# Feed-forwards and conv mixer of a two-layer decoder step as one level of Strassen block products

## The chip, the cores and the metric

One core of a Trainium2 chip runs the whole step in one launch. The metric is the device time of one execution in microseconds. Each time is the median of the runs shown with it; the profile is of one further execution.

## What is computed

Two groups of tokens (1024 prompt tokens; 8 sequences of 4 sample tokens) go through two layers with shared weights. What matters here is the part behind attention:

```python
def conv_mixer(h, prefix, w_in, conv_k, w_out):
    bg, cg, hv = jnp.split(h @ w_in, 3, axis=-1)
    u = cg * hv
    up = jnp.concatenate([prefix.astype(u.dtype), u], axis=1)
    y = sum(conv_k[j] * up[:, j:j + T] for j in range(CONV_WIDTH))
    return (bg * y) @ w_out, up[:, up.shape[1] - (CONV_WIDTH - 1):]

def swiglu(h, w_gu, w_down):
    g, u = jnp.split(h @ w_gu, 2, axis=-1)
    return (jax.nn.silu(g) * u) @ w_down
...
        hp = rms_norm(yp, norm2_g[i]) * (1.0 + sc2p) + sh2p
        yp = yp + g2p * swiglu(hp, ffn_w_gu[i], ffn_w_down[i])
```

Layer 0 is attention and a feed-forward, layer 1 the conv mixer and a feed-forward, then a last RMSNorm. D_MODEL is 1024, D_FF 2816, all in float32. The samples have the same formulas with their own conditioning.

## The kernel before

Model features lie on the 128 partitions (KT = 8 tiles), the 1056 tokens (T) along the free axis, in three chunks (NCH) of 352 (CH). float32 products are made of three fp32r products: weight and token are each split into a high part (an ACT copy to fp32r) and a low part (GpSimd: raw minus high), and `product` (L363 to L370, matmuls on L368) issues high x high, high x low and low x high for each k-tile into one PSUM bank.

The weights stream through a ring of four 128x1024 slots: SP loads `wraw` (`load_w`, L335; in the feed-forward loop L2280), ACT makes `uhi` (`split_hi`, L353), GpSimd makes `ulo` (`split_lo`, L360). Down weights have slots of their own (`draw`, `dhi`, `dlo`; L551, L556, L561).

Every engine runs its own program in the order in which it is written; semaphores tie them. Stages: projection, attention, `pe_out` (L2123: output projection, 24 items, item 16 on are the last), then `pe_ffn` (L2307) for ffn0, `pe_conv` (L2528), `pe_ffn` for ffn1, `pe_end` (L2719). A feed-forward has 11 iterations, each of two tiles of 128 hidden features: six units of a gate and an up product of 24 matmuls (`pe_ffn_unit`), then 24 down products of 6 matmuls (`pe_down`). ACT takes the gate from PSUM through SiLU (L2341), VectorE multiplies by up (L2452), ACT and GpSimd split the result (L2343, L2396), and VectorE adds the down product times the gate vector into the residual `y` in SBUF (`dve_down`, L582 to L591). The conv mixer has four such iterations of three products a tile (`pe_conv_unit`), with the three taps on VectorE (L2653, L2655).

The norm before a stage is made chunk by chunk under the products around it: squares on ACT (L395, L2157), sums over features by float32 matmuls with a matrix of ones (L407), mean (L471), root (L475) and reciprocal (L479), scale (L498), affine and high part on ACT (L522, L525), low part on GpSimd (L534, samples L539). At the end, nine token tiles are turned by matmuls (L2714), scaled from PSUM by VectorE (L2729) and ACT (L2736), and stored.

Of the kernel before, what the change touches and what calls it, by code (L numbers as in the profile page):

```python
# [14 lines left out]
P = 128  # L22
# [40 lines left out]
UP0 = {}  # L63
_at = 0
for _name, _n in (("proj", N_PROJ), ("out", N_OUT), ("ffn0", N_FFN), ("conv", N_CONV), ("ffn1", N_FFN)):
    UP0[_name] = _at
    _at += _n
MM0 = {"proj": 0, "out": 54, "ffn0": 54 + 3 * KT, "conv": 54 + 3 * KT + 6 * FT, "ffn1": 54 + 12 * KT + 6 * FT}
IT0 = {"ffn0": 0, "conv": 3 * FT, "ffn1": 3 * KT + 3 * FT}
# [82 lines left out]
CK0 = {"ffn0": 0, "conv": FT // 2, "ffn1": KT // 2 + FT // 2}  # L152


def program(nc, x_prompt, x_sample, c_prompt, c_sample, cache_k, cache_v, cache_kidx, state_conv, page_table,
# [6 lines left out]
    q_scr = nc.dram_tensor("q_scratch", [P, KT, T], F32, kind="Internal").ap()  # L162

    with ExitStack() as ctx:
# [6 lines left out]
        def layout(*specs):  # L171

            with ExitStack() as inner:
                return [inner.enter_context(nc.sbuf_tensor(n, s, d)) for n, s, d in specs]


        ident = sb("ident", [P, P])
        rotm = sb("rotm", [P, P])
# [2727 lines left out]
```

## Time and profile before

| | |
|---|---|
| median of 3 runs | 2795.92 us (2793.12 to 2799.52) |
| span of the profiled execution | 2797.2 us |
| from the first ffn0 product to the end | about 821 us to 2797 us of that span |
| busy share PE, PEld, VectorE, ACT, GpSimd | 97%, 89%, 42%, 30%, 33% |
| DMA, mean over the span | 69 GB/s |

PE is TensorE's matmuls, PEld its weight loads, DVE VectorE, POOL GpSimd, SPq the queue from which SyncE issues transfers. A group's "busy" counts each instruction from its start to its modelled end, so overlapping matmuls count twice; intervals between starts are the pace. "Idle before" is the time in which the engine had nothing to do before such an instruction, with what released it.

### The profile page before, as it was taken

The numbers are of one execution on the slowest core, as the hardware profiler recorded it, in microseconds if no ns is written. First come the engines' busy times: TensorE is split into PE (matmuls) and PEld (weight loads), VectorE is DVE, ScalarE is ACT, GpSimd is POOL, SyncE is SP. The second block draws the span as 40 slices with busy tenths as digits, with TensorE's granted clock in tenths as the row PEclk, the third lists the DMA queues.
The fourth block names the chain that finished last, engine by engine and source line by source line (L and its number), as shares of the span: only waits on it lengthen the run. The fifth ranks groups of instructions, "written<-read, shape, count | busy, mean of one in ns | idle before, by whom it ended". The sixth has DMA issues, their size and how long they took to land.

```text
span 2797.2 us, 46769 instructions
## 1 busy us (share of the span) xinstructions
PE 2711.9 (97%) x17946; PEld 2482.8 (89%) x17946; DVE 1173.9 (42%) x2915; ACT 850.2 (30%) x1622; POOL 919.6 (33%) x714
## 2 busy tenths in 40 slices
PE   6989999999999999999999999999999999999999
PEld 4848865767789999999999899999899999999999
DVE  5488988663263222222222443333622222222233
ACT  4156656772162111111111521111611111111113
POOL 3414643351054222222222533223532222222221
PEclk8999999999999999999999999999999999999999
DMA  8305567004321111111111012102111111111101
GB/s 305 84 24 164 172 235 224 2 1 134 99 76 46 46 45 45 45 45 45 45 45 45 16 45 61 46 16 61 46 46 45 45 45 45 45 45 45 45 15 64
DMA packets 206062, 192.23 MB, mean 69 GB/s; under 512 B 32480, under 2 KB 183880, under 8 KB 205418
## 3 DMA queue, kind: packets, MB, share of 16 engines
q1 hardware_dynamic: 205930, 190.42, 22.5%
q8 instruction: 88, 1.44, 0.2%
q14 instruction: 44, 0.36, 0.0%
HBM read 175.43 MB, written 14.96 MB: 68 GB/s over the span
## 4 chain that ended last, share of the span: by engine, by line
PE 88%; DVE 5%; ACT 2%; DMA 2%; issue 1%; POOL 1%; SPq 1%; DVEq 0%; ACTq 0%
PE PS L368 74%; PE PS L1880 3%; PE PS L1909 2%; PE PS L1891 2%; DVE s_all L1577 1%; DVE na L498 1%; PE PS L888 1%; DMA adaw<-in_ada_w_dram 1%; PE PS L407 1%; PE PS L901 1%; PE PS L2714 1%; ACT na L522 1%; PE PS L1896 1%; PE PS L1922 1%; POOL hlo L534 0%
## 5 line engine op out<-in xcount | busy, mean ns | idle before, releaser
L368 PE MATMUL PS<-hhi,uhi 128*128 128x352 f32 (+1 forms) x3240 | 1062.4, 328 | 19.2 <-DVE hlo L1306 7.3
L368 PE MATMUL PS<-hhi,ulo 128*128 128x352 f32 (+1 forms) x3240 | 1044.9, 323 | 0.0
L368 PE MATMUL PS<-hlo,uhi 128*128 128x352 f32 (+1 forms) x3240 | 1043.9, 322 | 0.0
L368 PEld LDWEIGHTS PS<-hhi,uhi 128*128 128x128 f32 (+1 forms) x3240 | 610.2, 188 | 39.3 <-issue 25.8
L368 PEld LDWEIGHTS PS<-hlo,uhi 128*128 128x128 f32 (+1 forms) x3240 | 612.0, 189 | 3.5 <-issue 0.2
L368 PEld LDWEIGHTS PS<-hhi,ulo 128*128 128x128 f32 (+1 forms) x3240 | 610.5, 188 | 0.8
L2396 POOL TENSOR_TENSOR alo<-af,ahi 128x352 fp32r<-128x352 f32 x132 | 126.0, 954 | 1023.1 <-ACT ahi L2343 1023.1
L2452 DVE TENSOR_TENSOR af<-sg,PS 128x352 f32<-128x352 f32 x132 | 68.8, 521 | 878.0 <-PE PS L368 872.6
L368 PE MATMUL PS<-ahi,dhi 128*128 128x352 f32 x1248 | 417.8, 335 | 4.7 <-DVE y L591 3.8
L368 PE MATMUL PS<-ahi,dlo 128*128 128x352 f32 x1248 | 402.6, 323 | 0.0
L368 PE MATMUL PS<-alo,dhi 128*128 128x352 f32 x1248 | 401.5, 322 | 0.0
L360 POOL TENSOR_TENSOR ulo<-wraw,uhi 128x1024 fp32r<-128x1024 f32 x124 | 294.8, 2397 | 65.4 <-ACT uhi L353 65.3
L582 DVE SCALAR_TENSOR_TENSOR y<-PS,mod,y 128x352 f32<-128x352 f32 x416 | 242.7, 584 | 157.2 <-PE PS L368 157.2
L2341 ACT ACTIVATE sg<-PS 128x352 f32<-128x352 f32 x132 | 61.3, 465 | 680.4 <-PE PS L368 680.4
L368 PEld LDWEIGHTS PS<-ahi,dhi 128*128 128x128 f32 x1248 | 233.8, 187 | 34.0 <-DVE y L591 26.8
L368 PEld LDWEIGHTS PS<-alo,dhi 128*128 128x128 f32 x1248 | 235.1, 188 | 2.2
L368 PEld LDWEIGHTS PS<-ahi,dlo 128*128 128x128 f32 x1248 | 234.4, 188 | 0.0
L2343 ACT ACTIVATE ahi<-af 128x352 fp32r<-128x352 f32 x132 | 65.8, 498 | 506.4 <-DVE af L2452 506.4
L585 DVE SCALAR_TENSOR_TENSOR y<-PS,mod,y 128x320 f32<-128x320 f32 x208 | 114.2, 549 | 48.6 <-PE PS L368 40.6
L353 ACT ACTIVATE uhi<-wraw 128x1024 fp32r<-128x1024 f32 x124 | 124.1, 1045 | 4.7 <-issue 4.7
L561 POOL TENSOR_TENSOR dlo<-draw,dhi 128x1024 fp32r<-128x1024 f32 x52 | 123.9, 2406 | 0.3 <-ACT dhi L556 0.2
L534 POOL TENSOR_TENSOR hlo<-na,hhi 128x352 fp32r<-128x352 f32 (+1 forms) x72 | 71.7, 996 | 119.6 <-ACT hhi L525 119.1
(303 smaller groups left out, 2817.0 us busy)
## 6 DMA issues: line engine op xcount, KB each, us to landing
wraw<-in_ffn_w_gu_dram SPq DMA_DIRECT2D x88, 512.0 KB, 7.4
wraw<-in_ada_w_dram SPq DMA_DIRECT2D x80, 512.0 KB, 4.5
draw<-in_ffn_w_down_dram SPq DMA_DIRECT2D x44, 512.0 KB, 4.3
wraw<-in_conv_w_in_dram SPq DMA_DIRECT2D x24, 512.0 KB, 7.1
adaw<-in_ada_w_dram SPq DMA_DIRECT2D x16, 512.0 KB, 14.4
wraw<-in_attn_w_out_dram SPq DMA_DIRECT2D x48, 128.0 KB, 3.1
y_scratch<-y SPq DMA_DIRECT2D x1, 4224.0 KB, 12.7
xst<-in_x_prompt_dram SPq DMA_DIRECT2D x4, 1024.0 KB, 8.5
```

Of the source, the lines that this page charges most:

```text
L353: act.activation(uhi[:, u % WR, :, 0:cols], wraw[:, slot, :, 0:cols], ACT.Copy).then_inc(up_hi, 1)
L360: pool.tensor_tensor(ulo[:, u % WR, :, 0:cols], wraw[:, slot, :, 0:cols], uhi[:, u % WR, :, 0:cols].bitcast(F32), ALU.subtract).then_inc(u ...
L368: last = pe.matmul(out, w(kt), x(kt), start=(n == 0), stop=(n == 3 * count - 1))
L534: pool.tensor_tensor(hlo[:, ft, cols_of(n)], nbufs(q)[1][:, k % 2, 0:width(n)], hhi[:, ft, cols_of(n)].bitcast(F32), ALU.subtract).then_in ...
L561: pool.tensor_tensor(dlo[:, b, :], draw[:, b, :], dhi[:, b, :].bitcast(F32), ALU.subtract)\
L582: dve.scalar_tensor_tensor(out=y[:, m, chunk(n)], in0=b[:, 0:CH], scalar=gate(m)[:, 0:1], in1=y[:, m, chunk(n)], op0=ALU.mult, op1=ALU.add ...
L585: dve.scalar_tensor_tensor(out=y[:, m, 2 * CH:SEQ], in0=b[:, 0:PC], scalar=gate(m)[:, 0:1], in1=y[:, m, 2 * CH:SEQ], op0=ALU.mult, op1=ALU ...
L1880: last = pe.matmul(wide(2 * g)[:, c], q_of(i, t)[64 * g:64 * g + 64], kT[64 * g:64 * g + 64, t // 4, c], start=True, stop=True)
L2341: act.activation(sg[:, p, :], bank[2 * p][:, 0:CH], ACT.Silu).then_inc(silu_rdy, 1)
L2343: act.activation(ahi[:, jj, chunk(n)], af[:, p, :], ACT.Copy).then_inc(act_hi, 1)
L2396: pool.tensor_tensor(alo[:, jj, chunk(n)], af[:, k % 2, :], ahi[:, jj, chunk(n)].bitcast(F32), ALU.subtract)\
L2452: dve.tensor_tensor(af[:, p, :], sg[:, p, :], bank[2 * p + 1][:, 0:CH], ALU.mult).then_inc(act_f, 1)
```

## The change

The three stages behind the output projection ("phases" ffn0, conv, ffn1) are rewritten for all engines. The constants now cut tokens into two groups of 528 (GS), each in two halves of 264 (H), and weights into two by two blocks. A two by two block product is made of seven products (the Winograd form), accumulated in PSUM in the order ORD with takes between: in all, an item has seven positions.

- A *U item* (up side) makes a pair of 128-feature tiles of gate or up (conv: c, h, b) for both halves of both token groups; PE runs 4 k-blocks x 3 matmuls x groups per position, 264 columns each. In the first and the last pair of a phase it is one item for each token group.
- Weight blocks of position 2 to 5 are sums made by VectorE (`dve_sums`); each position's 128x512 block is split by ACT (`act_split`) and GpSimd (`pool_split`) into one of four ring slots, four positions ahead. `lo_engine` gives all low parts to GpSimd but the first four of conv and ffn1.
- Results are taken by ACT (copies) and VectorE (adds, products) into rows of `y`, which is spilled to DRAM meanwhile (`sp_spill`) and reloaded (`sp_back`).
- The product of gate and up is cut into seven token pieces (`act_piece`, `pool_piece`, `dve_token_sums`), stored to DRAM through two stage buffers (`sp_piece`) and reloaded as tokens of the down side (`sp_tokens`).
- A *D item* (down side) makes half of the output features for four hidden tiles; feed-forwards have five chunks of two items, conv one. The hidden tiles left over are plain products (items P and Z, `pe_plain`, twelve matmuls each). At ffn's end that is one pair.
- The tokens of the next phase are built from the residual, 7 combinations by 4 k-blocks with high and low parts: group 0 during and behind Z (`act_z`, `dve_z`, `pool_z`), group 1 during the first pair's group 0 items (`act_build`, `dve_build`, `pool_build`). For ffn0, group 0's stand in `dve_out_proj`, `act_out_proj` and `pool_out`. The sums of squares move from PE to GpSimd (`pool_add`) with one small float32 product for each group (`pe_sum`).
- The tail's nine tiles are made in Z and behind it.

The diff, cut to its core:

```diff
-UP0 = {}
-_at = 0
...
+H = T // 4
+GS = 2 * H
+LAST = SEQ - GS
+ORD = (1, 2, 6, 5, 7, 3, 4)
+T_AT = {4: 0, 5: 1, 6: 2, 7: 3, 1: 4, 2: 5, 3: 6}
...
+PHASES = ("ffn0", "conv", "ffn1")
+KINDS = {"ffn0": "gu", "conv": "chb", "ffn1": "gu"}
+N_PAIRS = {"ffn0": FT // 2, "conv": KT // 2, "ffn1": FT // 2}
+N_CHUNKS = {"ffn0": 5, "conv": 1, "ffn1": 5}
...
+def lo_engine(p):
+
+    it, pos = ITEMS[PREP[p][0]], PREP[p][1]
+    if it.stage != "U":
+        return "pool"
+    first = IN_PHASE[it.phase][0].prep
+    if p < first + 4:
+        return "dve" if it.phase else "pool"
+    return "pool"
...
+                _who = ("act", "dve", "act", "act", "dve", "dve", "act" if _it.kind in "gc" else "dve")[_u]
...
+        def pe_u_item(pe, it):
+            fresh = it.at == 0 and it.kind == FIRST_KIND[it.phase]
+            for pos, i in enumerate(ORD):
+                r, w = it.res + pos, slot_of(it.prep + pos)
+                pe_split_ready(pe, it.prep + pos)
+                pe_bank_free(pe, r)
+                for s in it.groups:
+                    out, x = PS[:, 2 * SET[r] + s, 0:H], th[s][:, :, T_AT[i]]
+                    for k in range(4):
+                        if fresh:
+                            pe_tokens_ready(pe, it.phase, s, k, i)
+                        hi, lo = w[:, RH, P * k:P * k + P], w[:, RL, P * k:P * k + P]
+                        pe.matmul(out, hi, x[:, TH, k, :], start=(k == 0 and i in (1, 2, 5)), stop=False, skip_group_check=True)
+                        pe.matmul(out, hi, x[:, TL, k, :], start=False, stop=False, skip_group_check=True)
+                        last = pe.matmul(out, lo, x[:, TH, k, :], start=False, stop=(k == 3), skip_group_check=True)
+                last.then_inc(r_mm, 1)
...
+        def act_piece(act, n, k):
...
+            act.wait_ge(rd_d, PAIR_END[ph, j, 1 if s is None else s])
+            after(act, t_st[tp % 2], 16 * (tp // 2))
+            out = stages[tp % 2][:, TH, :]
...
+        def act_u_item(act, it):
+            for pos in range(7):
+                act_piece(act, it.n, pos)
+                act_take(act, it, pos)
+                act_silu(act, it, pos)
+                act_split(act, PREP_AT[it.n, pos])
+                if it.at == 0 and it.groups == (0,):
+                    act_build(act, it.phase, pos + (7 if it.kind in "uh" else 0))
...
+        def pool_split(pool, p):
+            if lo_engine(p) != "pool":
+                return
+            pool.wait_ge(w_hi, p + 1)
+            w = slot_of(p)
+            pool.tensor_tensor(w[:, RL, :], split_source(p), w[:, RH, :].bitcast(F32), ALU.subtract).then_inc(w_lop, 1)
...
+        def pool_build(pool, f, step):
+
+            if f == 0 and step == 0:
+                pool_add(pool, 0, 1, 7)
+            if step in (2, 4, 6, 8):
+                pool_low(pool, f, 1, step // 2 - 1, 1)
+            if step in (3, 5, 7, 9):
+                pool_lows(pool, f, 1, step // 2 - 1, (5, 6, 7, 4))
+
+        def pool_u_item(pool, it):
+            for pos in range(7):
+                pool_piece(pool, it.n, pos)
+                pool_split(pool, PREP_AT[it.n, pos])
+                if it.at == 0 and it.groups == (0,):
+                    pool_build(pool, it.phase, pos + (7 if it.kind in "uh" else 0))
...
+        def dve_t123(dve, f, s, k):
...
+            dve.tensor_tensor(t1, a[:, H:GS], a[:, 0:H], ALU.subtract).then_inc(n_t, 1)
+            dve.wait_ge(n_t, c + 1)
+            dve.tensor_tensor(t2, b[:, H:GS], t1, ALU.subtract).then_inc(n_t, 1)
+            dve.tensor_tensor(a[:, H:GS], b[:, H:GS], a[:, H:GS], ALU.subtract).then_inc(n_t, 1)
...
+        def dve_u_item(dve, it, late):
+
+            for pos in range(7):
+                p = PREP_AT[it.n, pos]
+                dve_split(dve, late)
+                dve_token_sums(dve, it.n, pos)
+                if it.kind == "b" and pos in (0, 2):
+                    dve_taps(dve, it, pos // 2)
+                dve_take(dve, it, pos)
+                dve_sums(dve, p + 1)
+                if it.at == 0 and it.groups == (0,):
+                    dve_build(dve, it.phase, pos + (7 if it.kind in "uh" else 0))
+                late = p
+            return late
...
             act_att(act)
             act_out_proj(act)
-            act_ffn(act, "ffn0", 1, 2, N_FFN + 4)
-            act_conv(act)
-            act_ffn(act, "ffn1", 3, 4, N_FFN)
+            for f in range(3):
+                act_phase(act, f)
             act_end(act)
```

## Rows read from the trace of the kernel before

**Rows 1.** The page's first part: busy time, share and instructions of each engine.

```profile
PE 2711.9 (97%) x17946; PEld 2482.8 (89%) x17946; DVE 1173.9 (42%) x2915; ACT 850.2 (30%) x1622; POOL 919.6 (33%) x714
```

**Rows 2.** The page's fourth part: the chain that ended last, by line.

```profile
PE PS L368 74%; PE PS L1880 3%; PE PS L1909 2%; PE PS L1891 2%; DVE s_all L1577 1%; DVE na L498 1%; PE PS L888 1%; DMA adaw<-in_ada_w_dram 1%; PE PS L407 1%; PE PS L901 1%; PE PS L2714 1%; ACT na L522 1%; PE PS L1896 1%; PE PS L1922 1%; POOL hlo L534 0%
```

**Rows 3.** Windows: stretch; its length, then busy us (instructions); clock, DMA share, GB/s.

```profile
821.00:1590.00 769.00, 766.84 (x4732) 753.01 (x4731) 226.27 (x512) 160.79 (x261) 249.73 (x161) 1.00 0.15 43
1590.00:1640.00 50.00, 45.62 (x262) 42.10 (x261) 31.79 (x61) 27.85 (x52) 22.83 (x21) 1.00 0.23 64
...
2755.00:2797.00 42.00, 36.32 (x287) 35.59 (x285) 19.01 (x47) 15.24 (x27) 6.78 (x8) 1.00 0.29 106
```

**Rows 4.** Timeline of PE (start, us, instruction): first and last of 26 matmuls.

```profile
1107.10 0.32 PE L368 MATMUL PS<-hlo,uhi 128*128 128x352 f32 x1
...
1111.07 0.32 PE L368 MATMUL PS<-hhi,ulo 128*128 128x352 f32 x1
```

**Rows 5.** Timeline of PE: first and last of 22 matmuls of 256 columns.

```profile
213.50 0.28 PE L368 MATMUL PS<-ulo,hhi 128*128 128x256 f32 x1
...
216.01 0.28 PE L368 MATMUL PS<-ulo,hhi 128*128 128x256 f32 x1
```

**Rows 6.** Timeline of ACT: SiLU takes, first and sixth of an iteration, first of the next.

```profile
1107.69 0.47 ACT L2341 ACTIVATE sg<-PS 128x352 f32<-128x352 f32 x1 [24.68 <-PE PS L368]
...
1145.76 0.47 ACT L2341 ACTIVATE sg<-PS 128x352 f32<-128x352 f32 x1 [2.50 <-PE PS L368]
1177.44 0.47 ACT L2341 ACTIVATE sg<-PS 128x352 f32<-128x352 f32 x1 [24.76 <-PE PS L368]
```

**Rows 7.** Timeline of PE in the out stage: sums between items 16, 17 and 18.

```profile
785.42 1.34 PE L407 MATMUL PS<-nsq,ones 128*128 128x352 f32 x4
790.42 1.34 PE L407 MATMUL PS<-nsq,ones 128*128 128x352 f32 x4
```

**Rows 8.** Groups of POOL by form: count, busy us, mean ns, idle before.

```profile
L360 POOL TENSOR_TENSOR ulo<-wraw,uhi 128x1024 fp32r<-128x1024 f32 x124 | 294.8, 2397 | 65.4 <-ACT uhi L353 65.3
L2396 POOL TENSOR_TENSOR alo<-af,ahi 128x352 fp32r<-128x352 f32 x132 | 126.0, 954 | 1023.1 <-ACT ahi L2343 1023.1
```

**Rows 9.** Groups of ACT by form.

```profile
L353 ACT ACTIVATE uhi<-wraw 128x1024 fp32r<-128x1024 f32 x124 | 124.1, 1045 | 4.7 <-issue 4.7
L2343 ACT ACTIVATE ahi<-af 128x352 fp32r<-128x352 f32 x132 | 65.8, 498 | 506.4 <-DVE af L2452 506.4
```

**Rows 10.** Groups of DVE by form.

```profile
L582 DVE SCALAR_TENSOR_TENSOR y<-PS,mod,y 128x352 f32<-128x352 f32 x416 | 242.7, 584 | 157.2 <-PE PS L368 157.2
L479 DVE RECIPROCAL rstd<-rstd 128x352 f32<-128x352 f32 x9 | 21.2, 2351 | 5.6 <-ACT rstd L475 5.6
```

**Rows 11.** Timelines of DVE (first row) and of POOL (the others) in the out stage.

```profile
793.15 2.69 DVE L498 TENSOR_TENSOR na<-y,rstd 128x352 f32<-128x352 f32 x1 [0.96 <-POOL hlo L534]
...
792.09 0.95 POOL L534 TENSOR_TENSOR hlo<-na,hhi 128x352 fp32r<-128x352 f32 x1 [0.53 <-ACT hhi L525]
793.05 2.41 POOL L360 TENSOR_TENSOR ulo<-wraw,uhi 128x1024 fp32r<-128x1024 f32 x1
795.40 1.22 POOL L534 TENSOR_TENSOR hlo<-na,hhi 128x352 fp32r<-128x352 f32 x1
```

**Rows 12.** Single lines L498 and L2452: duration min/median/max ns, first and last start.

```profile
L498 DVE TENSOR_TENSOR na<-y,rstd x72: 477/522/2685, 783.8 to 2020.5; 128x352 f32<-128x352 f32 x48, 128x320 f32<-128x320 f32 x24
...
L2452 DVE TENSOR_TENSOR af<-sg,PS x132: 520/522/523, 832.4 to 2752.6; 128x352 f32<-128x352 f32 x132
```

**Rows 13.** The chain that ended last, in order of time: start, us, what.

```profile
2782.18 10.84 PE PS L2714 x96
```

**Rows 14.** Windows, columns as in rows 3: a stretch after thin PE work.

```profile
388.00:400.00 12.00, 9.49 (x57) 4.25 (x57) 5.89 (x30) 4.53 (x21) 3.37 (x9) 0.51 0.97 357
```

**Rows 15.** DMA issues: count, KB each, median us to landing.

```profile
y_scratch<-y SPq DMA_DIRECT2D x1, 4224.0 KB, 12.7
...
q_scratch<-qst_ SPq DMA_DIRECT2D x21, 176.0 KB, 2.4
```

More of the change, by code:

```diff
@@ L62 @@
     _at += _n
-UP0 = {}
-_at = 0
[L65 to L69, printed above, removed]
+UP0 = {"proj": 0, "out": N_PROJ, "ffn0": N_PROJ + N_OUT}
+MM0 = {"proj": 0, "out": 54, "ffn0": 54 + 3 * KT}
 TOK = (0, P, CH - P)
@@ new lines, with outline @@
+Item = namedtuple("Item", "n phase stage kind at e groups prep ring res")
+PHASES = ("ffn0", "conv", "ffn1")
+KINDS = {"ffn0": "gu", "conv": "chb", "ffn1": "gu"}
+N_PAIRS = {"ffn0": FT // 2, "conv": KT // 2, "ffn1": FT // 2}
+N_CHUNKS = {"ffn0": 5, "conv": 1, "ffn1": 5}
+BOTH = (0, 1)
+def outline(name):
+    kinds, pairs = KINDS[name], N_PAIRS[name]
+    for j in range(pairs):
+        if j == 0 and name == "conv":
+            yield from (("U", k, j, 0, (s,)) for s in BOTH for k in "ch")
+            yield "U", "b", j, 0, BOTH
+        elif j in (0, pairs - 1):
+            yield from (("U", k, j, 0, (s,)) for s in BOTH for k in kinds)
+        else:
+            yield from (("U", k, j, 0, BOTH) for k in kinds)
+    for c in range(N_CHUNKS[name]):
+        yield from (("D", "", c, e, BOTH) for e in range(2))
+    if name == "conv":
+        yield "P", "", 2, 0, BOTH
+    yield "Z", "", pairs - 1, 0, BOTH
@@ new lines @@
+DVE_LO = list(itertools.accumulate(lo_engine(p) == "dve" for p in range(len(PREP))))
+SUM0 = {}
+for _it in ITEMS:
+    if _it.stage in "UD":
+        SUM0[_it.n] = 4 * len(SUM0)
+RAW_COUNT, _c = [], [0, 0]
+for _it in ITEMS:
+    _c[_it.n % 2] += 64 if _it.stage == "D" else 32
+    RAW_COUNT.append(_c[_it.n % 2])
+TAP_END, _c = {}, 0
+for _it in ITEMS:
+    if _it.stage == "U" and _it.kind == "b":
+        for _b in range(2):
+            _c += 3 + (1 if 0 in _it.groups else 0) + (2 if 1 in _it.groups else 0)
+            TAP_END[_it.n, _b] = _c
@@ new lines, with stage_done, v_row, t_op @@
+N_PIECES = _tp
+def stage_done(tp):
+    return [16 * ((tp + 1 - k) // 2) for k in range(2)]
+def v_row(f, pair):
+    return 6 if f == 1 or pair % 2 == 0 else 2
+def t_op(f, j):
+    done = [(g, k) for g in range(3) for k in range(2 * N_CHUNKS[PHASES[g]])]
+    return 4 * done.index((f, j))
+SQ0 = [0, 8, 16, 24, 33, 41, 50, 58]
+FIRST_KIND = {0: "g", 1: "c", 2: "g"}
+def lop(g, k, i):
+    at = (1, 5, 6, 7, 4).index(i)
+    if g == 0:
+        return 4 * k + at + 1 if i != 4 else 16 + k + 1
+    return 20 * g + 5 * k + at + 1
```

1885 lines of the change are left out of this document (1129 added, 756 removed).

## The prediction, made before the change was run

> **What bounds the kernel now.** I read the page's busy shares first: PE is busy 97% of the span, no other engine over 42% [rows 1]. The chain that ended last lies for 74% on the one line that issues every split product, L368 [rows 2]. By stretches, the first feed-forward keeps PE busy 766.8 of 769 us, the seam to the conv mixer 45.6 of 50, the tail 36.3 of 42 [rows 3]. So from 821 us to the end the kernel is matmul issue, and two prices matter: what a product costs PE, and what the other engines need once PE is quicker.
>
> PE's pace: 25 intervals of 352-column matmuls took 3.97 us, 158.8 ns each [rows 4]; 21 of 256 columns took 2.51 us, 119.5 ns [rows 5]. The difference, 39.3 ns for 96 columns, is one column per 0.41 ns; some 13 ns a matmul are fixed. 264 columns then cost 122.9 ns. In an iteration, five 48-matmul units take 38.07 us, the whole 432 take 69.75 [rows 6]; the 144 down matmuls between (69.75 - 38.07 - 7.63 = 24.05) cost 167 ns each, 50 ns extra per group of six.
>
> **The PE term.** Before: 2 x 11 x 69.75 = 1534.5 us for the feed-forwards, and 1728 x 0.159 + 576 x 0.167 = 371 for conv: 1906. After: a product position is 4 k-blocks x 3 matmuls x 2 token groups of 264 columns, 24 matmuls, 2.94 us; seven positions replace eight block products. Feed-forward: 22 item-equivalents x 168 = 3696, D 10 x 168 = 1680, the plain last pair 192: 5568 x 0.1226 = 683, and 140 x 0.05 for D's groups: 690. Conv: 2016 + 336 + 384 = 2736: 338. Together 1718, a gain of 188 us. The seventh of the work saved becomes a tenth of the time, since the fixed 13 ns are now paid 13872 times, not 11808.
>
> The Trainium skill (TensorE: Matmul & The Clock Gate, Back-to-back issue gap) gives columns / 2.4 + 2.5 ns as the isolated gap, 112.5 ns here, by which the PE term would be 144 us lower; it warns that this leaves out weight loads. For 352 columns it gives 149.2 where the row has 158.8, so the rows decide.
>
> **Who takes what else.** In the out stage (L2123) the 20 sums on PE between products go, 1.34 us for four [rows 7]; items 16 to 23 ran every 5.0 us there and need 3.82. I put item 16 at 778.5 and the stage's end at 810 (before: 821.4).
>
> Prices at the new sizes: GpSimd subtract or add, 2.15 ns an element between 352 and 1024: 0.76 us for 264 elements, 1.29 for 512, 1.33 for 528 [rows 8]. ACT copies 0.63 for 512, by the same slope method [rows 9]. VectorE from PSUM 0.78 for 528, reciprocal 1.78 for 264 [rows 10].
>
> The price I think decides: VectorE and GpSimd exclude each other where VectorE reads two SBUF operands. L498, 0.52 us at the median [rows 12], began at 793.15 and took 2.69, while a GpSimd subtract ran from 793.05 to 795.46; then the next GpSimd subtract took 1.22 instead of 0.95 [rows 11]. VectorE needed 0.38 us alone for 352 elements: 0.57 for 528, 0.55 for 512, 0.29 for 264. With one operand in PSUM it never waited: L2452 has 520/522/523 ns [rows 12]. So I add both engines' SBUF work as one queue, "the pair".
>
> The Trainium skill (SBUF — State Buffer, Who interferes with whom) also lets tensor_scalar and copies hold the pair; that would add only conv's first taps, some 8 us of pair time in an item with slack, and no time to the sum.
>
> **Middle pairs.** Per gate/up pair (PE 41.2 us): GpSimd 14 low parts 18.1 and 7 token pieces 9.3; VectorE 8 weight sums 4.4, 4 token sums 2.3, 3 products 1.7. Pair: 35.8, so PE still sets the pace. In the gate half it is 22.8 against 20.6. Following its start from the end of the last up position: five VectorE ops stand ahead of the take of position 1 (two weight sums, three token sums). Each finds GpSimd in a split (1.29) or a piece (1.33): weight sum done 2.55, token sum 4.5, weight sum 6.35, token sums 8.3 and 10.2 (three GpSimd ops between), take 10.9. PE wants that bank for position 3 at 8.8. I take 2 us a pair, 20 pairs: +40. From both sides: 0 (VectorE gets in first) and 3.5 (stores, below).
>
> **First pair of each phase.** Its items run one token group at a time, so weight splits are doubled, and the second group's tokens are built beside the first's products. Up to the second group's first product, GpSimd has 11 splits 14.2 and 20 low tokens 15.2, VectorE 15.5 on the pair (8 scalings 4.6, 12 sums 3.5, four high-low steps 3.4, weight sums and samples 4): 45 us where PE needs 20.6. After it, 14 splits and sums take 24 against 20.6: 3.5.
>
> **Seams.** In Z, VectorE's two reciprocals hold the last banks: 2.6. The next tokens need 20 low parts 15.2, two adds 2.7 and VectorE 10.9 = 28.8 of the pair after Z ends; with the chain scale, affine, high, low at its ends, 31.7 until splits go on. With 6 for dependencies: 2.6 + 31.7 + 45 + 6 + 3.5 - 20.6 = 68 a seam, twice: +136. Bounds: 50 if half of VectorE's work slips in while GpSimd waits for ACT, 85 if each k-block waits for its own chain.
>
> Out to feed-forward: from item 16 on, the pair has GpSimd 39.3 (add 1.3, four out splits 9.6, six adds 8, 20 low tokens 15.2, four splits 5.2) and VectorE 13.2: 52.5, then 46.2 as above. 778.5 + 98.7 + 5 + 3.5 - 20.6 = 865, 55 past the out stage's end. Bounds 40 to 70.
>
> **Last pair of each phase.** Four single-group items, PE 41.2; the pair has 22.8 (seven pieces of the pair before) + 12.1 + 13.9 + 12.1 = 60.9; the ring of four slots absorbs some: +17, conv the same with six items: +51 (36 to 60).
>
> **Tail.** Nine output tiles at 10.84 / 6 = 1.8 us [rows 13] and the last sums: 25 (22 to 30). **Clock.** After thin PE work TensorE's granted clock was 0.51 over 12 us, its lower level of 1.2 GHz [rows 14]; PE idles here at three starts: +8 (0 to 20).
>
> **New waits, and what is queued behind them.** PE waits per position for the low part of its ring slot (w_lop) and for its bank's last taker; all later products stand behind. VectorE waits before a take for ACT's copy of the partner (rd_a); weight sums for later slots stand behind. ACT waits before a token piece for the stage's store; its take, SiLU and split stand behind, and GpSimd's low part behind the split. SP waits for t_lo before a store; weight loads stand behind, needed an item later.
>
> **Edits costed at nothing.** ACT's splits, takes and pieces, 19 of 41.2 us a pair, behind PE; without that cover they would add their excess over 2.94 a position. SP's weight, token and spill transfers, one to four transfers ahead. y's reload, under the last group's items and D. VectorE keeps the first four low parts of phases two and three, inside Z.
>
> **Sum.** 810 + 1718 + 55 + 136 + 51 + 40 + 25 + 8 = 2843 us against this execution's span of 2797.2; the runs' median is 2795.9, so I forecast 2842.
>
> **Rivals.** (1) *The pair does not bind* (other side). If VectorE's short operations fall into GpSimd's waits for ACT, starts and seams are limited by GpSimd alone: the out start 30, seams 40 each, ends 25, middle 0, clock 5: 810 + 1718 + 30 + 80 + 25 + 25 + 5 = 2693; halfway 2768. It decides for faster once these extras come to under 262 us, against my 315. For it: all row averages have GpSimd at 33% [rows 1] with waits rare. Against: with both queued the rows show strict alternation [rows 11]. 0.23. (2) *The store round trip binds the middle.* A token piece's stage buffer returns only after its low part and a 528 KB store. Rows: 176 KB lands in 2.4 us, 4224 KB in 12.7 [rows 15], so 3.4 alone; two weight loads go out beside it. At 6 us the ACT take of position 6 comes 3.5 us late: 20 x 3.5 - 40 = +30 over my sum, and with slower seams +70: 2872 to 2913. For: ACT stands in order behind that wait, takes and splits queued after it. 0.17. (3) *It doesn't do what it says.* Before, all low parts are already on GpSimd, so "instead of VectorE" has no counterpart in this trace; what it adds to the pair is the 0.7 us a block by which GpSimd is slower, about 6 us per first pair, already in the sum. As a case without Strassen's effect I give it 0.02: 2797.
>
> **Chances and range.** Forecast 2843 (its own spread 2785 to 2875) 0.50, of which 0.02 lies on the faster side; rival 1 0.23; rival 2 0.17; within 0.2% 0.05, rival 3 in it; 0.05 slower than rival 2. A measurement of this kernel can tell some 0.2% from no change. Faster 0.25, same 0.05, slower 0.70. Range 2755 to 2935, which cuts the lower half of rival 1.
>
> **What would show it.** PE: L368's groups become 128x264 with starts 123 ns apart; about 2000 more matmuls. Gaps after each Z of 20 to 30 us on PE, released by GpSimd low tokens; in the first items GpSimd near 65% and VectorE ops of 1 to 1.9 us where 0.4 is their own. In a middle gate item one gap of 2 us before position 3, released by VectorE. If the gaps end on a DMA store, rival 2; if VectorE keeps its short durations, rival 1. I am wrong as a whole if PE's pace at 264 columns isn't 123 ns, or if a build takes 30 us, not 45.

## The result, and the profile after

The changed kernel takes 2810.6 us (median; 2803.6 to 2812.0) against 2797.5 us for the kernel before on the same chip, a ratio of 1.0047 (95% interval 1.0035 to 1.0059): slower, as forecast, but by 13 us and not by 45. Below, ratios are always to the kernel before, and 0.01 of ratio is 28 us. The profiled execution's span is 2810.2 us.

The page of the changed kernel: busy times, chain that ended last, then two groups of its fifth part and its two DMA rows of the token store.

```profile
PE 2539.0 (90%) x19876; PEld 2329.1 (83%) x19876; DVE 1862.9 (66%) x3186; ACT 1188.7 (42%) x2295; POOL 1682.9 (60%) x1278
...
PE 60%; DVE 12%; POOL 11%; DMA 6%; issue 5%; ACT 3%; SPq 1%; ACTq 0%; DVEq 0%; POOLq 0%
...
L2468 PE MATMUL PS<-th,ring 128*128 128x264 f32 x3136 | 923.6, 295 | 147.1 <-DVE y L2934 62.9
...
L2763 POOL TENSOR_TENSOR ring<-wraw,ring 128x512 fp32r<-128x512 f32 x364 | 536.5, 1477 | 261.5 <-ACT ring L2571 261.4
...
t_scratch<-stage SPq DMA_DIRECT2D x154, 528.0 KB, 3.1
th<-t_scratch SPq DMA_DIRECT2D x77, 1056.0 KB, 8.4
```

Where PE was busy 97% [rows 1], it is now busy 90%: its busy time fell by 173 us, and its idle time rose from 85 to 271 us. VectorE rose from 42% to 66% and GpSimd from 33% to 60%; the latter's 512-column pass takes 1.48 us on average, where the prediction priced it at 1.29 alone. The chain, which lay for 74% on one product line [rows 2], is now split among PE, VectorE and GpSimd.

Windows of the changed kernel, columns as in [rows 3]. In order: start of the first feed-forward, its middle pairs, its last pair, its down-projections, first pair of the second feed-forward with the seam ahead of it.

```profile
804.00:900.00 96.00, 57.67 (x342) 53.80 (x340) 75.24 (x100) 46.20 (x96) 76.31 (x65) 0.75 0.23 68
900.00:1279.40 379.40, 371.57 (x3025) 369.09 (x3026) 211.86 (x199) 162.67 (x280) 287.42 (x190) 1.00 0.44 141
1279.40:1343.00 63.60, 46.79 (x338) 45.05 (x337) 36.58 (x40) 28.18 (x57) 53.07 (x37) 0.90 0.82 298
1343.00:1550.50 207.50, 207.47 (x1681) 207.50 (x1682) 146.80 (x260) 46.37 (x75) 106.41 (x75) 0.99 0.60 218
...
2011.50:2107.50 96.00, 56.42 (x342) 52.55 (x340) 84.21 (x109) 54.58 (x115) 80.08 (x69) 0.79 0.22 66
```

From these I take an "excess": the time of a stretch less its matmuls at 0.1226 us each. 336 products are 41.2 us, so the start has 54.8 us of excess, the last pair 22.4, the middle 8.6 (3024 products, 370.8). The down-projections have none beyond 1.5 us. Over the up-projections of all three phases (item by item, from PE's timeline) the excess is 126 us in first pairs, 70 in last pairs, 26 in middle pairs. Before, the first feed-forward had 2 us of idle PE in 769 [rows 3].

PE's waits from 740 us on (total us, times, longest) say for whom.

```profile
PE PS L2468 <- DVE y L2934: 62.9, 50, 4.3
PE PS L2468 <- ACT y L2617: 37.9, 28, 4.7
PE PS L2536 <- issue: 28.6, 2, 14.3
PE PS L2468 <- issue: 24.4, 12, 7.4
PE PS L2468 <- POOL ring L2763: 12.4, 10, 4.6
PE PS L2490 <- DVE y L2934: 10.2, 3, 4.6
```

The first two are takes of finished products out of PSUM: in the up-projections PE waits mostly for a bank, not for weights (L2763 is only 12.4). L2536 is the norm's sum between two phases. The last row is the first down-product of each phase, and there the named take is only the last link. In the first feed-forward it stands in VectorE's program behind two weight sums, and these, like ScalarE's and GpSimd's splits of the same weights, waited for a transfer. Rows of ScalarE, VectorE and PE:

```profile
1340.02 1.15 ACT L2571 ACTIVATE ring<-wraw 128x512 fp32r<-128x512 f32 x2 [5.52 <-DMA wraw<-in_ffn_w_down_dram]
1340.03 0.69 DVE L2872 TENSOR_TENSOR sums<-wraw 128x512 f32<-128x512 f32 x1 [3.56 <-DMA wraw<-in_ffn_w_down_dram]
1342.47 0.41 DVE L2934 TENSOR_TENSOR y<-y,PS 128x264 f32<-128x264 f32 x1
1343.03 0.56 PE L2490 MATMUL PS<-th,ring 128*128 128x264 f32 x1 [4.59 <-DVE y L2934]
```

The DMA share is 0.82 over this last pair, where the middle pairs have 0.44. In the second feed-forward the same gap is 4.38 us. These 9 us are counted in the last pairs' 70.

The excess also holds the price of a lower clock. A window of the changed kernel from the end of a 4.30 us gap in the last pair (its row is in experiment 5), columns as above:

```profile
1288.24:1293.50 5.26, 5.26 (x24) 5.26 (x25) 1.22 (x1) 2.39 (x5) 5.26 (x5) 0.52 0.53 200
```

Here 24 matmuls took 219 ns each and not 122, at a granted clock of 0.52, the lower level of 1.2 GHz. In PE's timeline 132 intervals of the last pairs are of this kind (195 to 250 ns, no gap), 12.5 us together above 122.6 ns each; 276 are in first pairs (26.5 us) and 54 in middle pairs (4.3 us).

The pace itself: first and last row of 41 consecutive matmuls in PE's timeline.

```profile
1199.82 0.28 PE L2469 MATMUL PS<-th,ring 128*128 128x264 f32 x1
...
1204.70 0.28 PE L2470 MATMUL PS<-th,ring 128*128 128x264 f32 x1
```

4.88 us for 40 intervals: 122.0 ns for 264 columns, where [rows 4] and [rows 5] had given 122.9. The Trainium skill (TensorE: Matmul & The Clock Gate, Back-to-back issue gap) would have 112.5 by its formula for the isolated gap; the trace doesn't agree with it here.

### The profile page after: what moved, and what is told of

It is laid out like the page before. It is cut to its first block, busy times and chain, and to the rows that moved or that the text cites. A ratio compares the mean times of both kernels' runs of the same rounds, so it can differ in the third digit from the quotient of the medians.

```text
span 2810.2 us, 51944 instructions
## 1 busy us (share of the span) xinstructions
PE 2539.0 (90%) x19876; PEld 2329.1 (83%) x19876; DVE 1862.9 (66%) x3186; ACT 1188.7 (42%) x2295; POOL 1682.9 (60%) x1278
## 4 chain that ended last, share of the span: by engine, by line
PE 60%; DVE 12%; POOL 11%; DMA 6%; issue 5%; ACT 3%; SPq 1%; ACTq 0%; DVEq 0%; POOLq 0%
PE PS L572 9%; PE PS L2468 7%; PE PS L2470 7%; PE PS L2469 7%; PE PS L2490 5%; PE PS L2492 5%; PE PS L2493 5%; POOL ring L2763 5%; POOL stage L2776 4%; DMA t_scratch<-stage 3%; PE PS L1818 2%; PE PS L1847 2%; PE PS L1829 2%; POOL th L2791 2%; DVE s_all L1515 1%
## 5 line engine op out<-in xcount | busy, mean ns | idle before, releaser
L2468 PE MATMUL PS<-th,ring 128*128 128x264 f32 x3136 | 923.6, 295 | 147.1 <-DVE y L2934 62.9
L2470 PE MATMUL PS<-th,ring 128*128 128x264 f32 x3136 | 910.6, 290 | 0.0
L2469 PE MATMUL PS<-th,ring 128*128 128x264 f32 x3136 | 910.5, 290 | 0.0
L2468 PEld LDWEIGHTS PS<-th,ring 128*128 128x128 f32 x3136 | 610.3, 195 | 169.2 <-issue 134.9
L2763 POOL TENSOR_TENSOR ring<-wraw,ring 128x512 fp32r<-128x512 f32 x364 | 536.5, 1477 | 261.5 <-ACT ring L2571 261.4
L2469 PEld LDWEIGHTS PS<-th,ring 128*128 128x128 f32 x3136 | 611.3, 195 | 0.3
L2470 PEld LDWEIGHTS PS<-th,ring 128*128 128x128 f32 x3136 | 610.7, 195 | 0.0
L2763 POOL TENSOR_TENSOR ring<-sums,ring 128x512 fp32r<-128x512 f32 x269 | 408.9, 1524 | 197.5 <-ACT ring L2571 197.4
L2934 DVE TENSOR_TENSOR y<-y,PS 128x528 f32<-128x528 f32 (+1 forms) x207 | 122.9, 594 | 412.0 <-PE PS L2470 402.1
L2490 PE MATMUL PS<-th,ring 128*128 128x264 f32 x1232 | 353.4, 287 | 10.2 <-DVE y L2934 10.2
L2492 PE MATMUL PS<-th,ring 128*128 128x264 f32 x1232 | 352.4, 286 | 0.0
L2571 ACT ACTIVATE ring<-wraw 128x512 fp32r<-128x512 f32 x368 | 229.8, 626 | 288.8 <-PE PS L2493 200.4
L2493 PE MATMUL PS<-th,ring 128*128 128x264 f32 x1232 | 351.8, 286 | 0.0
L2571 ACT ACTIVATE ring<-sums 128x512 fp32r<-128x512 f32 x273 | 170.5, 629 | 416.5 <-DVE sums L2874 196.4
L2990 DVE SCALAR_TENSOR_TENSOR y<-PS,mod,y 128x528 f32<-128x528 f32 x308 | 235.4, 766 | 132.8 <-PE PS L2493 125.5
L2490 PEld LDWEIGHTS PS<-th,ring 128*128 128x128 f32 x1232 | 234.0, 190 | 10.7 <-POOL ring L2763 9.3
L2493 PEld LDWEIGHTS PS<-th,ring 128*128 128x128 f32 x1232 | 234.1, 190 | 0.0
L2492 PEld LDWEIGHTS PS<-th,ring 128*128 128x128 f32 x1232 | 233.9, 190 | 0.0
L2776 POOL TENSOR_TENSOR stage<-y,stage 128x528 fp32r<-128x528 f32 x110 | 184.9, 1681 | 51.6 <-ACT stage L2589 51.1
L572 PE MATMUL PS<-hhi,uhi 128*128 128x352 f32 (+1 forms) x552 | 191.2, 346 | 19.7 <-DVE hlo L1244 7.3
L572 PE MATMUL PS<-hhi,ulo 128*128 128x352 f32 (+1 forms) x552 | 182.6, 331 | 0.0
```

Source lines behind the costliest of these rows:

```text
L572: last = pe.matmul(out, w(kt), x(kt), start=(n == 0), stop=(n == 3 * count - 1))
L2468: pe.matmul(out, hi, x[:, TH, k, :], start=(k == 0 and i in (1, 2, 5)), stop=False, skip_group_check=True)
L2469: pe.matmul(out, hi, x[:, TL, k, :], start=False, stop=False, skip_group_check=True)
L2470: last = pe.matmul(out, lo, x[:, TH, k, :], start=False, stop=(k == 3), skip_group_check=True)
L2490: pe.matmul(out, hi, x[:, TH, 2 * k + s, :], start=(k == 0 and i in (1, 2, 5)), stop=False, skip_group_check=True)
L2492: pe.matmul(out, hi, x[:, TL, 2 * k + s, :], start=False, stop=False, skip_group_check=True)
```

## The experiments

Three theories are tested. *Pair*: VectorE's passes with two SBUF operands and GpSimd's passes take turns, and their joint work is late at the ends of each phase. *GpSimd alone*: rival 1. *Store*: ScalarE's wait for a token piece's store holds up takes (rival 2).

**1. Who takes turns with whom** (`sum64`, `lo64`). In `sum64` VectorE's four weight sums cover only the columns `c_ = slice(0, 64)` of 512 in up-projection items after the first (one of the four is shown); in `lo64` GpSimd's low parts of up-projection weights cover only `c = slice(0, 64)`, from the fifth ring position on. Both leave out most of what the kernel should compute there and serve only to measure time.

```
-                dve.tensor_tensor(a21, a11, a21, ALU.subtract).then_inc(w_sum, 1)
+                dve.tensor_tensor(a21[:, c_], a11[:, c_], a21[:, c_], ALU.subtract).then_inc(w_sum, 1)
...
-            pool.tensor_tensor(w[:, RL, :], split_source(p), w[:, RH, :].bitcast(F32), ALU.subtract).then_inc(w_lop, 1)
+            pool.tensor_tensor(w[:, RL, c], split_source(p)[:, c], w[:, RH, c].bitcast(F32), ALU.subtract).then_inc(w_lop, 1)
```

> The changed kernel with VectorE's four weight sums of each up-projection item made on 64 of 512 columns only (most of the sums is left out, the output is not the reference's); the down-projections keep theirs. Pair theory: about 4 x 0.5 us less of shared time in each of 26 one-group items, and the 1.8 us stretched passes of the middle get shorter: 30 to 50 us less, 2760 to 2780. GpSimd-alone theory: VectorE's passes don't matter, 2806 to 2812, and GpSimd's splits keep their mean of 1.48 us; by the pair theory they fall towards 1.3.

> The changed kernel with GpSimd's low parts of the up-projection weights made on 64 of 512 columns only (most of each low part is left out, the output is not the reference's); the down-projections keep theirs. Pair theory and GpSimd-alone theory alike: 7 us and more of GpSimd's time leave each one-group item, the stalls outside the token builds go, 60 to 100 us less, 2710 to 2750. If what is late is ScalarE (its copies, its takes behind the store wait) or the DMA of the weights, 15 us less at most, 2795 or more.

Measured: `sum64` 0.990 (0.988 to 0.992), 41 us below the changed kernel by the ratios; `lo64` 0.9765 (0.9744 to 0.9786), 79 us below. GpSimd alone would have given nothing for `sum64`, so that theory falls. The excess went from 126/70/26 (first, last, middle pairs) to 110/62/8 in `sum64` and to 90/52/0 in `lo64`. One part of `sum64`'s expectation failed: GpSimd's passes did not fall towards 1.3 us. Groups by form in `sum64`, of VectorE and GpSimd:

```profile
L2873 DVE TENSOR_TENSOR sums<-wraw 128x64 f32<-128x64 f32 x68 | 59.3, 873 | 3.1 <-DMA wraw<-in_conv_w_in_dram 1.8 <-DMA wraw<-in_ffn_w_gu_dram 1.2
L2877 DVE TENSOR_TENSOR wraw<-wraw 128x64 f32<-128x64 f32 x68 | 43.3, 637 | 0.0
...
L2763 POOL TENSOR_TENSOR ring<-wraw,ring 128x512 fp32r<-128x512 f32 x364 | 507.3, 1397 | 278.2 <-ACT ring L2571 275.5
L2763 POOL TENSOR_TENSOR ring<-sums,ring 128x512 fp32r<-128x512 f32 x269 | 396.9, 1479 | 184.3 <-ACT ring L2571 184.3
```

A VectorE pass over 64 columns still takes 637 to 873 ns on average. The shortest of these groups' passes took 0.21 us and the longest 1.31, so most of the average is a wait for the GpSimd pass under way. And GpSimd's mean falls only from 1477 to 1397 and from 1524 to 1479 (the down-projections, whose sums are whole, are in these groups too). So an eighth of the columns is far from an eighth of the price; the number of passes counts.

`lo64` also shows where the pair is not the cause. It takes some 22 us of GpSimd's time out of each feed-forward's last pair (28 passes of about 0.5 us instead of 1.29; an estimate from its groups of 454 and 551 ns), which leaves about 39 of the 60.9 us of pair work, less than PE's 41.2. Yet the two pairs keep 19.9 and 19.7 us of excess of 22.4 each; only conv's last pair falls, from 25.3 to 12.6. The longest gap of this pair in `lo64`'s first feed-forward is the one ahead of the down-products, where VectorE's weight sum waits for the down weights until 1314.78:

```profile
1317.79 0.56 PE L2490 MATMUL PS<-th,ring 128*128 128x264 f32 x1 [8.18 <-DVE y L2935]
```

**2. The order on ScalarE** (`takefirst`).

```
             for pos in range(7):
-                act_piece(act, it.n, pos)
                 act_take(act, it, pos)
                 act_silu(act, it, pos)
+                act_piece(act, it.n, pos)
```

> The changed kernel with one order turned round on ScalarE: in each up-projection position it first takes the finished product out of PSUM and then copies the token piece whose stage buffer is freed by a store, instead of the other way. Rival 2 of the prediction (the store round trip holds up ScalarE's takes): the gaps of 1.8 to 2 us at the first position of the both-group u items, seen in the changed kernel's trace, go, and about 0.4 to 0.6 of the 5.9 us gaps in the last pairs: 15 to 30 us less than the 2810.6 us of the changed kernel, 2781 to 2796. The pair theory (VectorE's two-operand passes and GpSimd's passes take turns, and their sum is what is late): ScalarE's order does not matter, 2807 to 2814.

Measured: 0.9974 (0.9964 to 0.9983), 20 us below the changed kernel and faster than the kernel before. All of it comes out of the middle: excess 126/72/0. ScalarE's waits ahead of the pieces between 900 and 1279 us (us, times), in the changed kernel and in this one:

```profile
  DMA t_scratch<-stage: 50.0, 24
  issue: 15.0, 15
```

```profile
  issue: 39.5, 25
  DVE y L2934: 3.4, 2
  DMA t_scratch<-stage: 0.4, 2
```

The waits fell from 65 us to 43 and did not vanish: what is left stands behind the take, where PE doesn't wait for it in these pairs. ("issue" names no releaser; that the store is behind these 39.5 us is not shown.) That agrees with the store theory, but the pair shows in the same edit. The same place in the changed kernel, a middle gate item after its start at 1196.0 us (DVE and POOL of the timeline):

```profile
1196.87 0.68 DVE L2876 TENSOR_TENSOR wraw<-wraw 128x512 f32<-128x512 f32 x1
1197.47 1.79 DVE L2897 TENSOR_TENSOR tA<-y 128x528 f32<-128x528 f32 x1
1199.19 1.82 DVE L2880 TENSOR_TENSOR sums<-wraw,sums 128x512 f32<-128x512 f32 x1
1200.94 1.79 DVE L2900 TENSOR_TENSOR tA<-y,tA 128x528 f32<-128x528 f32 x1
1202.65 1.82 DVE L2901 TENSOR_TENSOR y<-y 128x528 f32<-128x528 f32 x1
1204.40 0.69 DVE L2934 TENSOR_TENSOR y<-y,PS 128x528 f32<-128x528 f32 x1
...
1197.02 1.69 POOL L2763 TENSOR_TENSOR ring<-sums,ring 128x512 fp32r<-128x512 f32 x1 [0.25 <-ACT ring L2571]
1198.66 1.80 POOL L2776 TENSOR_TENSOR stage<-y,stage 128x528 fp32r<-128x528 f32 x1
```

and in the kernel with the take first (item from 1192.0 us):

```profile
1193.39 1.80 DVE L2897 TENSOR_TENSOR tA<-y 128x528 f32<-128x528 f32 x1
1195.11 0.68 DVE L2880 TENSOR_TENSOR sums<-wraw,sums 128x512 f32<-128x512 f32 x1
1195.71 0.70 DVE L2900 TENSOR_TENSOR tA<-y,tA 128x528 f32<-128x528 f32 x1
1196.33 0.70 DVE L2901 TENSOR_TENSOR y<-y 128x528 f32<-128x528 f32 x1
1198.02 0.70 DVE L2934 TENSOR_TENSOR y<-y,PS 128x528 f32<-128x528 f32 x1 [0.99 <-PE PS L2470]
...
1192.94 1.69 POOL L2763 TENSOR_TENSOR ring<-sums,ring 128x512 fp32r<-128x512 f32 x1 [0.24 <-ACT ring L2571]
1196.31 1.91 POOL L2776 TENSOR_TENSOR stage<-y,stage 128x528 fp32r<-128x528 f32 x1 [1.69 <-ACT stage L2589]
```

The same kinds of instruction on the same shapes take 0.68 to 0.70 us where GpSimd is idle or comes second, 1.79 to 1.82 where it has passes queued. Ahead of the take, ScalarE's copy of the piece started 1.0 us into the item; behind it, it starts at 3.6, GpSimd's piece therefore 4.3 and not 2.7, and three of VectorE's passes slip in ahead of it. The take ends 6.7 us after the item's start and not 9.1, and waits for PE instead of PE for it. One order on a third engine took both the store wait and the collision out of PE's way, so this run doesn't say how much of the 20 us belongs to each; in the changed kernel, 14.4 us of PE's 25.1 us of gaps in middle pairs are released by ScalarE and 10.7 by VectorE.

**3. Low parts on VectorE** (`share2`, `ends4`, `ends7`, `lows2`, `lows5`). The first three change the last line of `lo_engine` (one of the three lines below each), for items of the up-projections:

```
-    return "pool"
+    return "dve" if pos in (2, 5) else "pool"                                  # share2
+    return "dve" if len(it.groups) == 1 and pos in (0, 2, 4, 6) else "pool"    # ends4
+    return "dve" if len(it.groups) == 1 else "pool"                            # ends7
```

`lows2` and `lows5` leave the weights and give VectorE token low parts, in the builds after the first (with the waits on `n_lop` and `n_lod` recounted):

```
             for i in parts:
-                pool_low(pool, f, s, k, i)
+                if 2 * f + s == 0 or i not in LOV:      # LOV = (7, 4) or (1, 5, 6, 7, 4)
+                    pool_low(pool, f, s, k, i)
```

> The changed kernel with the low parts at positions 3 and 6 of each up-projection item on VectorE (two of seven), everything else as it is. Pair theory: each moved block takes 0.55 us of the shared time instead of 1.29, so 1.5 us less in each of the 26 one-group items where that sum is late and half of the 0.42 us stalls of the middle items: 20 to 35 us less, 2776 to 2791. GpSimd-alone theory: 2 x 1.5 us less of GpSimd in each one-group item, 35 to 60 us less. Rival (a block queued ahead of VectorE's takes, waiting for ScalarE's high part, holds up the PSUM banks): the middle stalls of 0.42 us grow to 1 us or more, 2820 to 2850.

> The changed kernel with the low parts at positions 1, 3, 5 and 7 of every one-group up-projection item (26 items, first and last pairs) on VectorE, GpSimd keeping all of the middle. Pair theory: 4 x 0.74 us less of shared time in each of the 26 items, of which the 14 of the last pairs can give back all of it (they are 5 us late each) and the 12 of the first pairs a part: 35 to 60 us less than 2810.6, 2750 to 2776. Rival (VectorE's own queue, waiting for ScalarE's high parts, becomes late instead): 0 to 15 us less, 2795 to 2811.

> The changed kernel with all seven low parts of every one-group up-projection item on VectorE. Pair theory: 7 x 0.74 = 5.2 us less of shared time an item, so the excess of the last pairs (70 us in 14 items) nearly goes and first pairs gain as well: 50 to 80 us less, 2730 to 2760, and better than with four of seven. Rival (VectorE's own length): 7 x 0.55 + 4 x 0.68 + its takes and products or build passes come near the 10.3 us of an item, so it is no better than four of seven, or worse, 2760 to 2800.

> The changed kernel with two of GpSimd's five low parts of each token row pair (parts 7 and 4, in the token builds after the first) on VectorE, the weights as they are. Pair theory: 8 parts x 0.47 us less of shared time in each of five builds, 19 us at most: 8 to 19 us less, 2792 to 2803. If the builds are late by their own chain (normalise, scale, sum, high part), 0 to 4 us less.

> The changed kernel with all five low parts of each token row pair on VectorE in the token builds after the first. Pair theory: 20 x 0.47 us in each of five builds, 47 us at most, 20 to 45 us less, 2766 to 2790. Rival (VectorE's own length in the builds): its passes grow by 20 x 0.29 us in each build and it waits in its queue for ScalarE's high parts, so no better than with two of five, 2795 to 2811.

Measured: `share2` 0.9992 (0.9977 to 1.0007), 15 us below the changed kernel; `ends4` 1.0012 (0.9999 to 1.0024), 10 below; `ends7` 0.9955 (0.9940 to 0.9970), 26 below; `lows2` 1.0065 (1.0040 to 1.0091), nothing gained; `lows5` 1.0025 (1.0009 to 1.0042), 6 below. Except for `lows2` the signs are the pair's, and seven of seven moved is better than four, but the sizes are a fifth to a half of those expected (`ends4` lies in its rival's range, and the 6 us of `lows5` are about the width of the intervals). In `ends7` the first pairs fell from 126 to 110 and the last from 70 to 58, 28 us for 26 items: 1.1 us an item where 5.2 us of pair work left it. So the joint work isn't the only thing late there. `lows2`'s zero fits the builds' own chain of normalise, scale, sum and high part, one of its two expected ends; no run tests that chain by itself.

**4. Do the edits add?** (`tf_ends7`, `tf_e7_l5`: `takefirst` with `ends7`, then with `lows5` too; their diffs are those above.)

> ScalarE's take first, and all low parts of the one-group items on VectorE. The two edits removed time in different places (the middle items, and the first and last pairs), so they should add: 23 and 27 us less than 2810.6, 2757 to 2764. If both had cured one common queue, 2775 to 2785.

> As the one before, and all five low parts of the token builds after the first on VectorE too. By themselves these gave 9 us; with GpSimd then empty of weight parts in the builds, pair theory: GpSimd has nothing left to take turns with in the first pairs, 10 to 20 us less than the one before, 2741 to 2753. Rival (VectorE's queue is now the longest in the builds): no gain or a loss, 2760 to 2775.

Measured: 0.9877 (0.9854 to 0.9899) and 0.9865 (0.9847 to 0.9883). By the ratios the first is 48 us below the changed kernel, the two parts 20 and 26: they add, as the places of the excess say: 1.7 us in middle pairs (`takefirst` alone 0), and 110 and 63 in first and last pairs (`ends7` alone 110 and 58). The token low parts add 3 us on top, within the intervals: not 10 to 20.

**5. Is a last pair late by order or by amount?** Take first left this gap in the last pair of the first feed-forward untouched, here in PE's timeline of the changed kernel and in that of `takefirst`:

```profile
1288.24 0.56 PE L2468 MATMUL PS<-th,ring 128*128 128x264 f32 x1 [4.30 <-DVE y L2934]
```

```profile
1282.68 0.56 PE L2468 MATMUL PS<-th,ring 128*128 128x264 f32 x1 [4.32 <-DVE y L2934]
```

The seven pieces of the pair before, which elsewhere go into an item of 20.6 us of PE time, fall into one of 10.3. `tf_spread` spreads them over two items (the condition in `dve_token_sums` follows, not shown), `tf_dtf` puts VectorE's take ahead of its token sums; `tf_all` and `tf_all_dtf` have these edits on top of `tf_e7_l5`, and `tf_e7_dtf` the order on top of `tf_ends7`.

```
-            PIECE_AT[_b.n, _k] = (_tp, _job)
+            _spread = _job[1] is not None and _b.kind == "g" and _b.groups == (0,)
+            PIECE_AT[((_b.n, _k), (_b.n, 4), (_b.n, 6), (_b.n + 1, 1), (_b.n + 1, 3))[max(_k - 2, 0)] if _spread else (_b.n, _k)] = (_tp, _job)
```

```
-                dve_token_sums(dve, it.n, pos)
                 if it.kind == "b" and pos in (0, 2):
                     dve_taps(dve, it, pos // 2)
                 dve_take(dve, it, pos)
+                dve_token_sums(dve, it.n, pos)
```

> ScalarE's take first, and the seven token pieces of the last both-group pair of each feed-forward spread over two one-group items (positions 1, 2, 3, 5, 7 of the g item and 2, 4 of the u item) instead of all in the g item. If the last pairs are late because seven pieces with their store round trips and 528-column passes, made for a 20.6 us item, fall into one of 10.3 us, the 23 us excess of each feed-forward's last pair falls to about 13: 15 to 25 us less than with take first alone (2787.5), 2763 to 2773. If it is the one-group items' own sums, splits and takes: 0 to 5 us less, 2782 to 2788.

> As the one before with the token pieces of the last both-group pair spread as well. If all of these add: 2726 to 2740. If the last pairs are already cured of what the spread cures: 2741 to 2753.

> ScalarE's take first, and on VectorE too: at each position the take of the finished product stands ahead of the token sums of that position. In the last both-group pair's pieces, g10s0 of the feed-forwards, five VectorE passes of 1.8 us stood ahead of the take of position 2, and the product at position 4 waited 4.3 us for its bank. If the order ahead of the take is what makes the last pairs late, two of the passes move behind it, the 4.3 us become about 0.8 in both feed-forwards: 6 to 9 us less than with ScalarE's take first alone (2777 to 2782 on the scale of 2787.5). If the last pairs are late by the whole amount of work in their four items, the gap reappears at the next take: 0 to 2 us less.

> The same order on VectorE, in the kernel with ScalarE's take first and all low parts of one-group items on VectorE (0.9877 of the kernel before). There the gap at position 4 is 3.35 us: if order is the cause, 5 to 8 us less, 0.985 to 0.986; if the amount of work is, 0.9877 again.

> The same order in the kernel with all edits (0.9845 of the kernel before: ScalarE's take first, one-group low parts and token low parts on VectorE, spread pieces). If order is the cause: 0.982 to 0.983, about 2747; if the amount of work is: 0.9845 again.

Measured: `tf_spread` 0.9972 (0.9959 to 0.9986) and `tf_dtf` 0.9969 (0.9956 to 0.9983), against 0.9974 for `takefirst`: nothing. `tf_e7_dtf` 0.9885 (0.9868 to 0.9903) against 0.9877: nothing. `tf_all` 0.9845 (0.9821 to 0.9869) and `tf_all_dtf` 0.9824 (0.9810 to 0.9838) are the fastest, and not told apart. In `tf_dtf` the 4.3 us gap did become 0.90, as worked out, and the excess of that last pair by item says where it went (us, from PE's timeline):

| | g, group 0 | u, group 0 | g, group 1 | u, group 1 | sum |
|---|---|---|---|---|---|
| `takefirst` | 8.0 | 7.7 | 2.4 | 5.2 | 23.3 |
| `tf_spread` | 7.9 | 3.2 | 4.8 | 6.3 | 22.2 |
| `tf_dtf` | 6.2 | 9.3 | 2.4 | 4.6 | 22.5 |
| `tf_all` | 4.6 | 2.1 | 6.2 | 6.0 | 18.8 |

Each stall that goes comes back two to ten positions later, so a last pair isn't late by the order of VectorE's or ScalarE's work alone. But the amount of pair work isn't shown to be the cause either: `tf_e7_l5`, which has the same low parts moved as `tf_all` but no spread pieces, has 22.5 us in this pair, and `lo64` kept 19.9 with far less pair work. Limits stand in a row here, and each experiment that eases one uncovers the next. One of them is the landing of the down weights: its gap is 4.59 us in the changed kernel, 4.77 in `takefirst`, 4.62 in `tf_spread`, 4.14 in `tf_dtf`, 5.82 in `tf_all` and 8.18 in `lo64`, most of the excess of that last u item (in `lo64` 8.3 us). No run issues those loads earlier, so that remedy stands untested. With the kernel before at 2796 to 2798 us in these comparisons, the best version, at 2749.3 (0.9824), beats it by 1.8%, and the changed kernel by 2.2%.

## Why the prediction was right or wrong

The sign held, and so did the place of nearly every loss: PE's work fell about as priced, and the other engines' work at the ends of each phase took back more. The sum came out 33 us too high. Five terms were too large (PE -12, out stage -6, seams -12, middle pairs -13, clock -8) and one too small (last pairs +19), so the misses partly cancelled, which is luck. The step that failed in its mechanism is "I take 2 us a pair" for the middle pairs, from the order followed: that gap was 0.42 us, and the larger part of the loss there was ScalarE's wait for the store. Next come two sizes: the seams, and the 50 ns a group on the down-projections. And the last pairs' sum had nothing for a late weight load and for the clock. From 2843 to the span of 2810:

- **PE's pace and work**: 122.0 ns for 264 columns, forecast 122.9; 1930 more matmuls, forecast about 2000. The extra 50 ns per group of the down-projections nearly vanished: 207.5 us for each feed-forward's, where 213 were counted (1680 matmuls at 0.1226 us are 206.0), in all -12 us. Right in the main price, wrong in carrying a per-group cost from [rows 6] to other groups.
- **Out stage**: ended at 803.9, forecast 810 (-6). **Start**: 54.9 of excess, forecast 55.
- **Seams**: about 55 us each plus 7 each in the last plain steps: 124, forecast 136 (-12). Both builds follow the turn-taking from [rows 11]; DVE and POOL of the changed kernel's timeline in the first pair:

```profile
852.51 1.26 DVE L3101 TENSOR_TENSOR th<-tB,th 128x528 fp32r<-128x528 f32 x1
853.70 0.96 DVE L3105 TENSOR_TENSOR tB<-tB,t 128x264 f32<-128x264 f32 x1
854.59 1.23 DVE L2876 TENSOR_TENSOR wraw<-wraw 128x512 f32<-128x512 f32 x1
...
852.32 2.05 POOL L2791 TENSOR_TENSOR th<-t,th 128x264 fp32r<-128x264 f32 x2 [0.82 <-ACT th L2700]
854.33 2.09 POOL L2791 TENSOR_TENSOR th<-tB,th 128x264 fp32r<-128x264 f32 x2
```

  Passes that the sum priced at 0.29 to 0.57 us, and that take 0.42 (264 columns) to 0.69 where they run alone, take 0.96 to 1.26. That the total came out so close is partly luck: `lo64` shows 90 of the 126 us of first-pair excess still there with most of GpSimd's weight work gone, so the sum of the pair's work isn't what sets all of it, although the sum gave the right time. Of the other part, the chain through ScalarE and the 26.5 us of slow-clock intervals are candidates that no run separates.
- **Middle pairs**: 26 us in all, forecast 40 (-13). The hand-followed order put one gap before position 3 of the gate item, released by VectorE, at 2.1 us; it is there, at 0.42, since a weight sum got in ahead of GpSimd and the take ended at 9.1, not 10.9. But more than half of the loss sat behind the first positions of the u items, released by ScalarE, which waits for the store: rival 2, to which I had given 30 us more and a chance of its own. It was real and small, 0.8 us a pair, and it was the cheapest to remove. It isn't a rival but a partner.
- **Last pairs**: 70, forecast 51 (+19), the largest miss. For a feed-forward's last pair I had 60.9 us of pair work and let the ring of four slots absorb 3; it took 63.6. That this is near the sum is luck too: with a third of the pair work gone, `lo64` kept 19.9 and 19.7 of the 22.4 us. What the sum had at nothing for these pairs is in the trace: PE waited 4.59 and 4.38 us at the first down-products, behind SyncE's weight loads, which were among the "edits costed at nothing", and the lower clock took 12.5 us in these pairs, 21 us together where the miss is 19. How much of either would come back if it were removed, no run shows.
- **Tail** 24 for 25. **Clock**: the granted clock is 0.75 and 0.79 in the two starts' windows above, and 336 products of 41.2 us occupy PE for 57.7 and 56.4 us. I had added 8 us for it; in the starts PE waits for the builds anyway, and what it cost in the last pairs is counted there, so it has no line of its own (-8).
- **Rival 1** (GpSimd alone) falls with `sum64`. **Rival 3** (the change without effect, 2797) falls too: PE's busy time fell by 173 us. Where the low parts are made does matter a little: two of seven on VectorE (`share2`) are 15 us better than none of seven.

## What to carry to other kernels

When a change removes a seventh of the bounding engine's work, price what the others need at the joints (first and last items, seams), where their work doubles or their time halves: here 173 us saved on PE came back as 186 us of idle time. Put the instruction that frees a shared buffer first in each engine's order and those that wait for a transfer behind it; that cost nothing and gave 20 us. Judge the removal of a stall by the sum over its whole stage: here a gap of 4.3 us became 0.90 and the pair's 23.3 us became 22.5. And follow a gap past the releaser that the profile names to what that one waited for: here a weight load.

## What the runs showed of the hardware

- VectorE passes with two SBUF operands wait for the GpSimd pass under way, short ones too: 64 columns took 0.21 us at the least, 1.31 at the most and 637 to 873 ns on average; 512 columns took 0.68 alone and 1.8 in turns. The Trainium skill (SBUF — State Buffer, Who interferes with whom) tells of such sharing between the two engines; the trace agrees.
- GpSimd's own passes wait in turn: 512 columns took 1.28 us alone and 1.69 to 1.76 in turns with long VectorE passes. In the item at 1196.0 one turn of both engines took 1.74 us, less than the 1.29 + 0.55 of the sum: these lengths contain the other engine's part and don't come on top of it.
- A take with one operand in PSUM (1204.40 above) ran in 0.69 us, its own length, in the middle of such a chain of turns.
- After a 4.30 us gap PE's granted clock was 0.52, the lower of its two levels (1.2 GHz), over 5.26 us, and matmuls of 264 columns started 219 ns apart instead of 122.
